# Block 2's attention probabilities and state output: from TensorE transposes to VectorE 32x32 blocks and a scratch in HBM

## The reference, cut to what matters

```python
u = rmsnorm(h, mix_norm); z = u @ w_in
m_qk, m_v, m_o, m_i, m_f, a_q, a_k, a_v, g_m, g_a = split(z)
m_qk = silu(causal_dwconv(m_qk, m_conv_w, m_conv_b))
hm = sigmoid(m_o) * head_rmsnorm(mlstm_chunkwise(m_q, m_k, m_v, m_i, log_sigmoid(m_f)))
aq, ak = head_rmsnorm(a_q), head_rmsnorm(a_k)                 # 16 query heads, 4 kv heads, 64 wide
ha = swa_gqa_sinks(aq, ak, a_v, a_sinks)                      # window of 128, softmax with a sink
merged = sigmoid(g_m) * (hm @ w_branch_m) + sigmoid(g_a) * (ha @ w_branch_a)
h = h + merged @ w_out
```

## Time and profile before

| what | us |
|---|---|
| median of three runs (2297.05 to 2297.55) | 2297.5 |
| the profiled execution's own time | 2293.15 |
| its span, first to last instruction | 2291.4 |
| TensorE busy | 2278.3 |
| VectorE busy | 1533.0 |
| ScalarE busy | 1232.8 |
| GpSimd busy | 134.6 |

### The profile page before, as it was taken

The page is one execution under the profiler, slowest core; times in us unless marked ns, Lnnn a source line. Parts: engine busy times, 40 slices in busy tenths (PEclk is TensorE's granted clock), DMA queues, the critical chain, the costliest instruction groups (busy, mean ns, idle before and its releaser), DMA issues.

```text
span 2291.4 us, 30120 instructions
## 1 busy us (share of the span) xinstructions
PE 2278.3 (99%) x11144; PEld 1902.6 (83%) x11144; DVE 1533.0 (67%) x2411; ACT 1232.8 (54%) x1890; POOL 134.6 (6%) x141
## 2 busy tenths in 40 slices
PE   9999999999999999999999999999999999999999
PEld 8887888888888888888888888888888888888887
DVE  6667786566687866676487666664765687657654
ACT  6556444445555444355467754554544477645443
POOL 3140000013220000000000000000000000000000
PEclk9999999999999999999999999999999999999999
DMA  8556568756485587487564444875677564456772
GB/s 337 197 181 257 192 230 293 225 184 211 148 293 192 184 278 240 164 274 248 188 232 154 165 153 160 270 244 195 220 239 239 180 221 157 148 175 204 233 238 87
DMA packets 179857, 483.08 MB, mean 211 GB/s; under 512 B 20480, under 2 KB 65152, under 8 KB 178688
## 3 DMA queue, kind: packets, MB, share of 16 engines
q1 hardware_dynamic: 179712, 481.16, 62.8%
HBM read 452.24 MB, written 28.84 MB: 210 GB/s over the span
## 4 chain that ended last, share of the span: by engine, by line
PE 94%; DVE 3%; DMA 1%; ACT 1%; issue 1%; SPq 0%; DVEq 0%; ACTq 0%
PE bank L2113 28%; PE bank L2118 27%; PE bank L2117 27%; PE bank L2160 2%; PE bank L2100 2%; PE bank L2101 2%; PE bank L2102 2%; DMA raw<-in_weights 1%; DVE wl L1602 1%; PE bank L2249 1%; PE bank L2211 0%; PE bank L2182 0%; PE bank L2234 0%; ACT wh L1372 0%; SPq L1190 0%
## 5 line engine op out<-in xcount | busy, mean ns | idle before, releaser
L1372 ACT ACTIVATE wh<-raw 128x1024 fp32r<-128x1024 f32 (+1 forms) x778 | 813.6, 1051 | 774.7 <-PE bank L2118 684.1
L1602 DVE TENSOR_TENSOR wl<-raw,wh 128x1024 fp32r<-128x1024 f32 (+1 forms) x778 | 932.7, 1229 | 271.0 <-ACT wh L1372 267.8
L2113 PE MATMUL bank<-wh,xh 128*128 128x512 f32 (+1 forms) x2102 | 825.8, 393 | 5.3 <-issue 4.0
L2118 PE MATMUL bank<-wh,xl 128*128 128x512 f32 (+1 forms) x2102 | 815.9, 388 | 0.0
L2117 PE MATMUL bank<-wl,xh 128*128 128x512 f32 (+1 forms) x2102 | 814.9, 388 | 0.0
L2113 PEld LDWEIGHTS bank<-wh,xh 128*128 128x128 f32 x2102 | 394.7, 188 | 86.9 <-issue 7.8
L2118 PEld LDWEIGHTS bank<-wh,xl 128*128 128x128 f32 x2102 | 394.5, 188 | 81.1
L2117 PEld LDWEIGHTS bank<-wl,xh 128*128 128x128 f32 x2102 | 394.9, 188 | 77.1
L2113 PE MATMUL bank<-wh,act_h 128*128 128x512 f32 x528 | 205.9, 390 | 0.0
L2118 PE MATMUL bank<-wh,act_l 128*128 128x512 f32 x512 | 199.3, 389 | 0.0
L2117 PE MATMUL bank<-wl,act_h 128*128 128x512 f32 x512 | 199.3, 389 | 0.0
(11 more groups left out here) (347 smaller groups left out, 2068.5 us busy)
## 6 DMA issues: line engine op xcount, KB each, us to landing
raw<-in_weights SPq DMA_DIRECT2D x760, 512.0 KB, 4.3
turn<-ffn_s SPq DMA_DIRECT2D x264, 64.0 KB, 2.8
ffn_a<-turn SPq DMA_DIRECT2D x66, 256.0 KB, 4.6
raw<-in_weights SPq DMA_DIRECT2D x16, 384.0 KB, 3.4
ln<-in_ln SPq DMA_DIRECT2D x4, 1024.0 KB, 7.5
moved<-merged SPq DMA_DIRECT2D x32, 128.0 KB, 6.6
merged<-moved SPq DMA_DIRECT2D x8, 512.0 KB, 5.3
bias<-in_bias SPq DMA_DIRECT2D x2, 1024.0 KB, 8.6
```

The lines of the kernel that those rows point to most:

```text
L1372: act.activation(wh[:, u % NH, 0:used(u)], raw[:, u % NR, 0:used(u)], ACT.Copy).then_inc(hi_done, 1)
L1602: dve.tensor_tensor(wl[:, u % NR, 0:used(u)], raw[:, u % NR, 0:used(u)], wh[:, u % NH, 0:used(u)].bitcast(F32), ALU.subtract).then_inc(lo_ ...
L2113: pe.matmul(out, h, w_h, start=st.first and i == 0, stop=False)
L2118: last = pe.matmul(out, lo, w_h, start=False, stop=ends)
```

## The change

- In block 2 the probabilities of a pair of heads are scaled by GpSimd (two multiplications, in place), turned in 32x32 blocks by VectorE (one instruction of 128x768), written to the scratch in four DMAs and read back in one; `aa_pv` reads them from there, in runs of 32 columns. TensorE's 48 transposes a layer, ScalarE's scaling and its copies to `PT` are gone.
- The state output `mo` goes by `block`, `out`, `back`, `halve`, in place of 16 transposes a layer.
- The pieces of `Pn` are stored in another order (query rows 0 to 127 first).
- `weave` takes a place for each side step, counted in dense units that stand ahead of it. A pair's steps stand at its place plus 0 (`aa_s`), 2 (`even`), 4 (`block`), 5 (`out`), 7 (`back`) and 10 (`aa_pv`) units (`PAIR_STEPS`).
- `m_rows` and the `m_arow` steps stand earlier; `m_rows` is now directly ahead of the last pair's `aa_s`.
- The reciprocal root of the queries is a step of its own (`a_root`), behind `conv 0`. The query half `aq1` is turned later.
- In block 1, the steps of the differential attention (`da_s`, `da_mix`, `da_pv`) stand up to one unit later.

```diff
+PAIRS_AT = (6, 9, 12, 15, 18, 21, 25, 28)
+PAIR_STEPS = (("pv", 10), ("back", 7), ("even", 2), ("s", 0), ("block", 4), ("out", 5))
...
-    def weave(self, before, dense, side, table):
...
+    def weave(self, before, dense, side, places):
+
+        assert len(places) == len(side), (len(places), len(side))
         self.steps = before
...
+        left = sorted(zip(places, side), key=lambda pair: pair[0])
+        done = 0
+        for st in dense:
+            if st.kind == "unit":
+                while left and left[0][0] <= done:
+                    self.steps.append(left.pop(0)[1])
...
+                done += 1
+            self.steps.append(st)
+        self.steps += [sd for _, sd in left]
...
     p.add("m_log", t=p.next_t(), c=c_log)
     for r in range(R):
         p.add("a_sum", tile=r)
-    for name in ("ak", "aq0", "aq1"):
-        if name == "aq1":
-            p.moved("back", name)
-        c_a = p.moved("copy", name)
+    p.add("a_root")
+    for name in ("ak", "aq0"):
+        p.moved("copy", name)
+    for what in ("block", "out", "back", "copy"):
+        c_a = p.moved(what, "aq1", kept=q["aq1"], m=p.cc["copied"] - 1)
...
-    q["o"] = heads(p, "aa", AH // 2, scores, q["akv"])
-
-    p.add("m_rows", s=p.next_s())
+    done, evens = {}, {}
+    for _, _, what, pair in sorted((at + after, k, what, pair) for pair, at in enumerate(PAIRS_AT)
+                                   for k, (what, after) in enumerate(PAIR_STEPS)):
+        h = 2 * pair
+        if what == "s" and pair == AH // 2 - 1:
+            p.add("m_rows", s=p.next_s())
+        if what == "s":
+            done[h] = scores(h)[1]
...
-    t_m = split_rows("mo", "hm", KT, rows=p.cc["rows"])
+    for what in ("block", "out", "back", "halve"):
+        for r in range(R):
+            h_m = p.moved(what, f"mo{r}", rows=p.cc["rows"], dst="hm", tile=r)
...
+                    elif st.kind == "even" and st.of == "aa":
+                        n = st.h
+                        pool.wait_ge(shares, st.m)
+                        for r in (1, 0):
+                            part = b["Pn"][:, n % 4:n % 4 + 2, 128:384] if r else b["Pn"][:, n % 4:n % 4 + 2, 0:128]
+                            last = pool.tensor_tensor(part, part, of2(rc, n)[:, 2 * r:2 * r + 2].unsqueeze(2)
+                                                      .broadcast_to([P, 2, 256 if r else P]), ALU.mult)
+                        last.then_inc(evened, 2)
...
+                    elif k == "block" and st.name.startswith("pair"):
+                        dve.wait_ge(evened, st.m)
+                        dve.transpose(stage[st.name].rearrange("p (q m n) -> p q m n", q=4, m=6),
+                                      b["Pn"][:, st.h % 4:st.h % 4 + 2, :].rearrange("p a n -> p (a n)")
+                                      .rearrange("p (m q n) -> p q m n", m=6, q=4)).then_inc(blocked, 1)
...
-                        turned(st.t)
+                        if k == "ca_pv":
+                            turned(st.t)
+                        else:
+                            pe.wait_ge(moved_back[st.name], 16 * (st.l + 1))
```

More of the change, by code:

```diff
@@ L169, in begin @@
         return kept
-    def weave(self, before, dense, side, table):
[L173 to L184, removed]
-        self.steps = before
[L186 to L192, removed]
+    def weave(self, before, dense, side, places):
+        assert len(places) == len(side), (len(places), len(side))
+        self.steps = before
+        left = sorted(zip(places, side), key=lambda pair: pair[0])
[4 more added lines that the diff above has]
+                    self.steps.append(left.pop(0)[1])
+                assert not any(sd.t is not None and sd.t == st.after_t for _, sd in left), st.u
+                assert not any(sd.kind == "o_split" and sd.o + 1 == st.after_o for _, sd in left), st.u
+                done += 1
+            self.steps.append(st)
+        self.steps += [sd for _, sd in left]
     def flip(self):
@@ L690, in plan_block2 @@
     p.moved("back", "aq0")
-    p.moved("out", "aq1")
     p.add("p_split")
@@ L735, in scores @@
         return p.count("soft"), p.count("soft")
-    q["o"] = heads(p, "aa", AH // 2, scores, q["akv"])
-    p.add("m_rows", s=p.next_s())
+    done, evens = {}, {}
[6 more added lines that the diff above has]
+            done[h] = scores(h)[1]
+        elif what == "even":
+            evens[pair] = p.count("even", 2)
+            p.add("even", h=h, of="aa", soft=done[h], m=p.count("shares"))
+        elif what == "block":
+            p.moved("block", f"pair{pair}", h=h, m=evens[pair])
+        elif what in ("out", "back"):
+            p.moved(what, f"pair{pair}", h=h)
+        else:
+            if h % 4 == 0:
+                q["o"] = p.next_o()
+            p.add("aa_pv", h=h, o=q["o"], name=f"pair{pair}", kept=q["akv"])
+            if h % 4 == 2:
+                p.add("o_split", h=h, o=q["o"], dst="ha", n=p.count("hi"), m=p.count("o_ready_0"))
     arow = {}
@@ L1138, in build @@
                  "aq0": b["merged"][:, 0, :],
-                 "aq1": b["merged"][:, 1, :]}
+                 "aq1": b["mo"][:, 1, :]}
+        flat = b["merged"][:, :, :].rearrange("p r n -> p (r n)")
+        for i in range(AH // 2):
+            stage[f"pair{i}"] = (flat[:, 0:768], flat[:, 768:1536], b["PT"][:, :, :].rearrange("p a n -> p (a n)"))[i % 3]
         landed = {**stage,
@@ L1377, in _ @@
                                        scale=st.scale).then_inc(t_hi, 1)
-                    elif k == "even" and st.of == "aa":
-                        act.wait_ge(shares, st.m)
-                        for i in range(2):
-                            for r in (1, 0):
-                                part = b["Pn"][:, (st.h + i) % 4, 0:256] if r else b["Pn"][:, (st.h + i) % 4, 256:384]
-                                at = 2 * (st.h % 8) + 2 * r + i
-                                last = act.activation(part, part, ACT.Copy, scale=rc[:, at:at + 1])
-                            last.then_inc(evened, 1)
                     elif k == "o_split":
```

72 lines of the change are left out of this document (41 added, 31 removed), and 3 rows, old and new, of the table PLACES_2.

## The result

| | us |
|---|---|
| changed kernel, median of four runs (2312.72 to 2315.04) | 2313.64 |
| kernel before, median of four runs | 2297.28 |
| ratio, 95% interval | 1.0078, 1.0064 to 1.0092 |
| profiled execution of the changed kernel, and its span | 2313.91, 2312.2 |

What follows compares the result with a forecast made beforehand. TensorE, busy 99% of the span, was taken to bound the kernel. The terms -7.3 + 0.8 - 1.9 + 6 + 1.5 + 0.5 gave -0.4 us a layer, -0.8 for two: from 2297.5 to about 2297, range 2285 to 2310.

Steps and rivals of the forecast that it cites:

- d: Gate rows ahead of the last pair's scores, sharing bank SB: TensorE waits for VectorE's copies, +6 us a layer, bounds 1.3 and 8.
- a: Block 2: TensorE's 48 transposes and the 16 of `mo` go, -7.3 us a layer.
- b: Block 2: scores and value products stand apart, four more borders a layer on TensorE, +0.8 us a layer.
- c: Root moved behind `conv 0`: TensorE's idle time at unit 407 goes, -1.9 us a layer, bounds 0 and -2.0.
- e: Scores of heads 6 and 7 wait for VectorE to read SB, +1.5 us a layer, bounds 0 and 3.5.
- f: Pair 0's way through the scratch delays its value product, +0.5 us a layer, bounds 0 and 2.6.
- GpSimd holding VectorE: Rival: GpSimd's scalings delay VectorE by 1.8 us each, +5.4 a layer, 2307 us; chance 0.15.
- The value product in runs of 32 columns: Rival: reading its moving operand this way doubles the value product's time, 6.6 us a layer, 2310 us; chance 0.05.
- The scratch: Rival: scratch data late for every pair, eight value products wait 2 to 3 us each, 2330 us and more; chance 0.08.
- VectorE keeps up: Rival: at the gate rows only a 1.3 us round trip remains, e and f are 0, 2283 us; chance 0.30.

Runs made afterwards that it cites:

- experiment 9: Changed kernel with ScalarE's exponentials as a step of their own one unit behind the scores, gate rows where the change put them: 2290.5 us, 0.9982.
- experiment 10: Kernel before, with ScalarE's exponentials as a step of their own one unit behind the scores, nothing else: 2296.2 us, 1.0001.
- experiment 7: Changed kernel with gate rows behind the last pair's scores and ScalarE's exponentials as a separate step one unit after the scores: 2278.5 us, 0.9933.
- experiment 11: The kernel of experiment 7 with the reciprocal root of the queries back ahead of `conv 0`: 2281.5 us, 0.9939.
- experiment 3: Changed kernel with the reciprocal root of the queries back ahead of `conv 0`, all else the same: 2312.0 us, 1.0072.
- experiment 6: Kernel before, with only the gate rows moved directly ahead of the last pair's scores: 2305.2 us, 1.0047.
- experiment 4: Changed kernel with the steps of heads 12 and 13 one unit earlier (24 for 25): 2318.2 us, 1.0097.

## Why the prediction was wrong

**The step that failed is d**, "Let time 0 be the end of heads 12 and 13's scores", from which VectorE was to start with the masks at once, or "2.9 late". It started 6.7 late. The rest of d's working holds: it gave the copies' end 16.3 after time 0, and 16.3 + 6.7 is 23.0; it came at 1288.8 - 1265.9 = 22.9. TensorE was forecast at 11.3 and came at about 12. The wait was 10.8 where I took 6 and had 8 as the bound. The 6.7 are ScalarE's order at work earlier in the stage: in experiment 9, where only that order differs, VectorE starts 1.2 after the scores, and the wait is 3.7. I had worked out the stretch and not the state in which the engine enters it, though the side steps ahead of it (the output gate, `o_split`, pairs of scores three units apart) were all in the order. The scores of heads 12 and 13 also stand ahead of `conv 6` now and stood behind it before, so their exponentials are in front of its first taps.

**What no step had: ScalarE.** I priced it as losing work. Its busy time did fall, but its order counts. In d I did set the exponentials ahead of the first taps, and did not see that this happens at `conv 2` too, nor that it could be undone. With the exponentials one unit later the changed kernel goes from 2313.6 to 2290.5, and with the gate rows later from 2303.0 to 2278.5; in the kernel before the same edit is worth nothing. The four kernels show two costs that nearly add: 23 to 25 us for ScalarE's order (22 by the ratios) and 11 to 12 for the place of the gate rows (11 by the ratios). Both hold what the lower clock costs behind the waits.

**a and b are confirmed** as far as they can be: between the experiments 10 and 7, which differ by the change and the place of the gate rows, lie 17.7 us (15.6 by the ratios); a, b and c made 2 x (7.3 - 0.8 + 1.9) = 16.8. The reordering in block 1 is in that difference too, and no run takes it out.

**c**: its mechanism is right, the wait at unit 407 is 0.23 for 1.97, and comes back with the root. What it left out is where the root's work goes. Its worth depends on that: 3.0 in experiment 11, nothing in the changed kernel, where the wait came out at unit 415 (experiment 3).

**e** was at the wrong place. The scores of heads 6 and 7 wait for nothing; 3.0 a layer come at unit 415 by way of `conv 2`, ahead of these scores, and with the lower clock behind it that held TensorE up by 4.6. VectorE was done with the masks of heads 4 and 5 at 1228.7, and the scores came at 1230.0.

**f** is right: one wait of 0.4 for a DMA, in one layer.

**The lowered clock** was in no term: 3.6 a layer behind waits of 3.0 and 10.8. It may also be in the 4.35 us by which the profiled execution of the kernel before was faster than its median. That execution has 1.000 behind both waits of 2.0. Others of the same kernel, beside experiment 10, have a granted clock from 1.000 (spans of 2290.5 to 2292.1) to 0.998 (2296.1 and 2296.2); only their means are on record, so where they lose it is not shown.

**The rivals.** GpSimd holding VectorE is not what made the kernel slower: without its work the time is the same, though TensorE's waits are 3.3 shorter in two layers (its two multiplications took 2.5, where I had put 1.8). The rule that I drew from the Trainium skill (page "SBUF — State Buffer", section "Who interferes with whom") would have made 2307; the lengthened low part of 1.80 agrees with it. The price here is small, as most low parts do not fall beside a scaling and VectorE's idle time takes up part of the rest. The value product in runs of 32 columns did not double: from its start to the next unit's first product it is 0.80 in the changed kernel (1233.82 to 1234.62), as before (1218.14 to 1218.94), and experiment 7 leaves no room for 13 us. The scratch was late by 0.4 once (f). "VectorE keeps up" was right of the change's inner worth and is the time of experiment 7, 2278.5 against the 2283 that I gave it; it needs ScalarE's order to be mended.

**Open**: why the lower clock follows a wait in one place and not in another. Behind the wait of 2.0 at unit 407 it came in both layers of experiment 6, in layer 0 of experiment 10 and not in its layer 1, and not in the profiled execution of the kernel before.

## What to carry to other kernels

When a change takes work from the engine that bounds, every order on the other engines that it used to hide comes to light: look at what is queued behind each of their waits, and above all behind an instruction that waits for a late neighbour while data for the next ones lie ready. A wait at the end of a stage must be worked out with the lateness at the stage's start; if that is unknown, it belongs in the range. And test a suspected wait by moving the thing, not by its size: the waits at units 407 and 415 could be removed one by one without any gain, since the two engines behind them kept their pace.

## What the runs showed of the hardware

TensorE's granted clock was 0.50 (1.2 GHz) for a stretch behind each wait of 3.0 us and more that was read here. In the changed kernel the twelve products behind the wait of 3.03 took 4.30 us for 2.73, so a wait of 3.0 cost 4.6; in experiment 9 it was ten products in layer 0 and four in layer 1 behind the same wait of 3.7. Just below that it goes both ways. In experiment 4 the clock was 0.50 behind the wait of 2.96 in layer 0 and 1.00 behind that of 2.98 in layer 1. Behind waits of 2.0 at unit 407 it was 1.00 in both layers before and in layer 1 of experiment 10, and 0.50 in both layers of experiment 6 and in layer 0 of experiment 10. So the length of the wait alone does not decide it.

Side by side with a GpSimd multiplication, a two-input VectorE addition of 128x1024 took 1.80 us when it started second, and 1.20 when it started 0.16 ahead.
